# Three transformer layers on one core: loads moved between queues, a 16-row bias table, the ends of three mixers in another order, and no dummy products

## The reference

```python
def gmlp_mixer(x, ...):
    z = gelu(x @ w_in); u, v = split(z)
    v = layernorm(v, ln_g, ln_b)
    v = einsum('gpq,bnqgc->bnpgc', masked(w_s), v) + b_s
    return (u * v) @ w_out

def diff_attention(x, ...):
    s = q @ k.T * scale + rel_bias[t5_bucket(kpos - qpos)]   # two maps of each head
    attn = softmax(s0) - lam_full * softmax(s1)
    o = rmsnorm(attn @ v, sub_g) * (1 - lambda_init)
    return o @ w_out

def conv_ffn(x, ...):
    h = causal_dwconv(x @ w_up, conv_w, conv_b)
    return (gelu(h[..., :2816]) * h[..., 2816:]) @ w_down

for layer in (0, 1):
    h = h + rmsnorm(mixer(rmsnorm(h, g0)), g1)
    h = h + rmsnorm(conv_ffn(rmsnorm(h, g2)), g3)
x = h + 0.5 * swiglu(rms_norm(h))
x = x + concat(mla(...), moba(...)) @ w_out
x = x + 0.5 * swiglu(rms_norm(x))
return rms_norm(x)
```

## Time and profile before

| | before |
|---|---|
| median of 3 runs | 1166.54 us (1165.56 to 1166.56) |
| the profiled execution | 1168.31 us, its span 1166.1 us |
| mean granted clock of TensorE | 0.975 |
| PE, DVE, ACT, POOL busy | 94%, 63%, 52%, 3% of the span |
| read from DRAM | 195.35 MB, 170 GB/s over the span |

### The profile page before, as it was taken

The page is one execution under the profiler, slowest core; times in us unless marked ns, Lnnn a source line. Parts: engine busy times, 40 slices in busy tenths (PEclk is TensorE's granted clock), DMA queues, the critical chain, the costliest instruction groups (busy, mean ns, idle before and its releaser), DMA issues.

```text
span 1166.1 us, 18036 instructions
## 1 busy us (share of the span) xinstructions
PE 1096.7 (94%) x7308; PEld 1002.7 (86%) x7308; DVE 732.7 (63%) x1145; ACT 607.7 (52%) x1060; POOL 40.5 (3%) x47
## 2 busy tenths in 40 slices
PE   6989399999899898999999999999998989999997
PEld 4977399999789777999997999999897978999996
DVE  4865297767768875876767654555546845655453
ACT  6655166555756655655556543435453644543442
POOL 0720010000000000000000000000000000000000
PEclk9999699999999999999999999999998989999999
DMA  9742677565374234656554566565353422855540
GB/s 334 244 172 64 137 251 230 171 195 183 108 261 154 91 109 133 229 179 198 168 196 127 193 216 200 169 198 192 107 173 123 150 72 69 277 179 189 191 162 37
DMA packets 56081, 199.14 MB, mean 171 GB/s; under 512 B 6856, under 2 KB 7272, under 8 KB 56000
## 3 DMA queue, kind: packets, MB, share of 16 engines
q1 hardware_dynamic: 54000, 194.53, 50.2%
q0 software_dynamic: 1088, 2.63, 1.5%
q10 hardware_dynamic: 912, 0.84, 0.2%
HBM read 195.35 MB, written 2.62 MB: 170 GB/s over the span
## 4 chain that ended last, share of the span: by engine, by line
PE 85%; DVE 6%; ACT 4%; DMA 3%; issue 1%; ACTq 0%; DVEq 0%
PE Y L1242 26%; PE G L1207 15%; PE G L1209 15%; PE G L1208 15%; DMA raw<-in_panels 3%; DVE w_low L733 2%; PE G L1230 2%; PE G L1232 2%; PE G L1231 2%; ACT w_high L384 1%; PE G L1365 1%; PE Y L1254 1%; PE Y L1208 1%; PE Y L1207 1%; PE Y L1209 1%
## 5 line engine op out<-in xcount | busy, mean ns | idle before, releaser
L733 DVE TENSOR_TENSOR w_low<-raw,w_high 128x1024 fp32r<-128x1024 f32 x352 | 428.1, 1225 | 109.3 <-ACT w_high L384 108.0
L1207 PE MATMUL G<-x_parts,w_high 128*128 128x256 f32 x1504 | 429.7, 286 | 1.1 <-DVE w_low L733 1.1
L1208 PE MATMUL G<-x_parts,w_high 128*128 128x256 f32 x1504 | 427.9, 285 | 0.0
L1209 PE MATMUL G<-x_parts,w_low 128*128 128x256 f32 x1504 | 427.7, 284 | 0.0
L384 ACT CAST w_high<-raw 128x1024 fp32r<-128x1024 f32 x352 | 359.1, 1046 | 47.2 <-DMA raw<-in_panels 32.3
L1207 PEld LDWEIGHTS G<-x_parts,w_high 128*128 128x128 f32 x1504 | 290.6, 193 | 5.4 <-issue 2.1
L1208 PEld LDWEIGHTS G<-x_parts,w_high 128*128 128x128 f32 x1504 | 290.6, 193 | 2.9
L1209 PEld LDWEIGHTS G<-x_parts,w_low 128*128 128x128 f32 x1504 | 290.4, 193 | 0.0
L1242 PE MATMUL Y<-w_high,a_high 128*128 128x512 f32 x448 | 144.6, 405 | 25.4 <-DVE a_low L849 21.9
L1242 PE MATMUL Y<-w_high,a_low 128*128 128x512 f32 x448 | 142.2, 399 | 0.0
L1242 PE MATMUL Y<-w_low,a_high 128*128 128x512 f32 x448 | 141.6, 398 | 0.0
(11 more groups left out here) (211 smaller groups left out, 952.7 us busy)
## 6 DMA issues: line engine op xcount, KB each, us to landing
raw<-in_panels SPq DMA_DIRECT2D x352, 512.0 KB, 4.5
gain_pre<-in_gains SPq DMA_DIRECT2D x7, 512.0 KB, 5.6
gain_post<-in_gains SPq DMA_DIRECT2D x4, 512.0 KB, 6.8
rel_rows<-qk POOLq DMA_DIRECT2D x1, 1536.0 KB, 34.6
big<-in_xT SPq DMA_DIRECT2D x4, 256.0 KB, 9.0
h<-in_x SPq DMA_DIRECT2D x2, 512.0 KB, 13.8
big<-rel_rows POOLq DMA_DIRECT2D x8, 128.0 KB, 3.3
out_y<-w SPq DMA_DIRECT2D x4, 256.0 KB, 2.0
```

The source lines that it names most:

```text
L733: v.tensor_tensor(WL[:, n % RING, :], raw[:, n % RAWS, :], WH[:, n % RING, :].bitcast(F32), ALU.subtract).then_inc(lo, 1)
L1207: mm(out, WH[:, j, c:c + w], xh, start=first, stop=False, skip_group_check=skip)
L1208: mm(out, WH[:, j, c:c + w], xl, start=False, stop=False, skip_group_check=skip)
L1209: return mm(out, WL[:, j, c:c + w], xh, start=False, stop=last, skip_group_check=skip)
```

## The change

It does eight things. Loads: the six small loads move from ACT's queue to SP's, between the first panels; panel 5 comes ahead of `h`. Bias table: 16 rows a head, written by POOL as soon as `relt` is there and read back by SP in 8 pieces of 16 partitions, one behind every fourth panel of FFN0 from FFN0+6. FFN: the first `d` one pair of tiles later; conversions of panels +5 to +8 beside the `first2` copies; with the convolution a tile waits for `taps` and not for the product. Boundaries: panel +3 is converted within the boundary, except before FFN3, where it stays ahead. GMLP end: the mixing in two halves. DIFF end: norms of heads 0 to 3 ahead of `evac_qk(7)`, then those of 4 to 7 together; rows t=0 of heads 0 to 2 ahead of t=1. MIX: the evacuation and scores of pair 8 ahead of the rest, MoBA and MLA tiles one place later. No `warm`.

The parts stand in the order of the file: `_ffn_order`, SP, POOL, ACT (boundary, `first_two`, `ffn`, start, DIFF end), DVE (GMLP end, DIFF end, MIX), PE.

```diff
-        if 3 <= f < NF - 2:
-            seq.append(("d", f - 3))
+        if 4 <= f < NF - 1:
+            seq.append(("d", f - 4))
...
-        scratch = nc.dram_tensor("rel_rows", [HEADS, P * REL], F32)
+        scratch = nc.dram_tensor("rel_rows", [HEADS, 16 * REL], F32)
...
             load(4)
+            sp.dma_start(relw, io["rel"]).then_inc(rel_in, 16)
+            load(5)
             for t in range(TT):
                 sp.dma_start(h[:, t, :], io["x"][t]).then_inc(x_in[t], 16)
-            load(5), load(6)
+            load(6)
+            sp.dma_start(cst[:], io["consts"]).then_inc(cst_in, 16)
+            load(7)
             sp.dma_start(wsT, io["w_s"]).then_inc(ws_in, 16)
-            load(7)
+            sp.dma_start(par[:], io["params"]).then_inc(par_in, 16)
+            load(8)
             sp.dma_start(bsrow, io["b_s"].to_broadcast([P, D])).then_inc(ws_in, 16)
+            load(9)
+            sp.dma_start(posi[:, 0:T], io["pos_row"].to_broadcast([P, T])).then_inc(pos_in, 16)
+            sp.dma_start(posi[:, T:T + TT], io["pos_col"]).then_inc(pos_in, 16)
+            def table_rows(a):
+                src = bass.AP(scratch, P - 1 - 16 * a, [[REL - 1, 16], [16 * REL, HEADS], [1, T]])
+                sp.dma_start(bias[16 * a:16 * a + 16, :, P:SC], src).then_inc(rel_rd, 16)
...
+                if n == FFN0 + 2:
+                    sp.wait_ge(vp_r, 2)
+                    sp.wait_ge(rel_wr, 16)
+                    sp.dma_start(lamrow[:].rearrange("p a b -> p (a b)"),
+                                 io["lam"].to_broadcast([P, 4 * DIFF_D])).then_inc(lam_in, 16)
+                if n >= FFN0 + 6 and (n - FFN0 - 6) % 4 == 0 and n < FFN0 + 6 + 32:
+                    table_rows((n - FFN0 - 6) // 4)
                 load(n)
...
+            pool.wait_ge(relt_r, 1)
+            pool.dma_start(scratch_ap.rearrange("e (r c) -> e r c", c=REL),
+                           relt[:].unsqueeze(1).to_broadcast([HEADS, 16, REL])).then_inc(rel_wr, 16)
             pool.wait_ge(ws_in, 32)
...
-            pool.wait_ge(used, FFN0 + 4)
-            pool.dma_start(scratch_ap.rearrange("e (r c) -> e r c", c=REL),
-                           relt[:].unsqueeze(1).to_broadcast([HEADS, P, REL])).then_inc(rel_wr, 16)
-            pool.wait_ge(rel_wr, 16)
-            pool.wait_ge(vp_r, 1)
-            for e in range(HEADS):
-                src = bass.AP(scratch, e * P * REL + P - 1, [[REL - 1, P], [1, T]])
-                pool.dma_start(bias[:, e, P:SC], src).then_inc(rel_rd, 16)
-            pool.wait_ge(rel_rd, 16 * HEADS)
+            pool.wait_ge(rel_rd, 16 * 8)
...
+                upto(base + 3)
                 h_rms(b, 1)
...
                     s.copy(first2[:, t, :], G[:, t, :]).then_inc(fx_r, 1)
+                    upto(base + 7 + t)
...
-                upto(base + 5)
+                upto(base + 4)
-                upto(base + 3 * NF + 3)
+                upto(base + 3 * NF + 2)
...
-            upto(4)
+            upto(6)
             h_rms(0, 0)
-            upto(5)
             h_rms(0, 1)
             preload(ACT.Gelu_apprx_tanh)
             upto(9)
...
-                if k == HEADS - 1:
-                    rms_out(0, 5, 1)
-                    preload(ACT.Exp)
                 if k >= 1:
                     exps(k - 1)
                 if k >= 2:
                     last = squares_out(k - 2)
-                    if k == 6:
+                    if k == 5:
                         last.then_inc(ac, 1)
+                if k == 6:
+                    rms_out(0, 4, 1)
+                    preload(ACT.Exp)
             high_head(0), high_head(1)
+            turned_out(6, 0)
             exps(7)
-            turned_out(6, 0)
-            turned_out(7, 0)
+            high_head(2)
             squares_out(6)
             upto(DIFF + 31)
-            high_head(2)
+            turned_out(7, 0)
+            high_head(3)
             squares_out(7).then_inc(ac, 1)
-            rms_out(5, HEADS, 2)
+            rms_out(4, HEADS, 2)
...
+            mixed_in(0, 4)
             for k in range(4):
                 gate(k)
             for k in range(4):
                 a_low(k)
-            upto(21)
             scale_u(3)
+            mixed_in(4, KT)
             gate(4), gate(5)
+            upto(20)
             a_low(4), a_low(5)
             gate(6), gate(7)
+            upto(21)
             a_low(6), a_low(7)
...
+                if k == HEADS - 1:
+                    inverse_rms(0, 4, 1)
+                    for e in range(4):
+                        norm_head(e)
                 evac_qk(k, DIFF + 10 + 2 * k, DIFF_D ** -0.5)
-                upto(DIFF + 15 + 2 * k)
+                if k < HEADS - 1:
+                    upto(DIFF + 15 + 2 * k)
...
-                    inverse_rms(0, 5, 1)
-                    norm_head(0), norm_head(1)
                     head_values(5)
-                    combine(7)
...
+            combine(7)
             low_head(0), low_head(1)
+            head_values(6)
             weigh(7)
-            norm_head(2)
-            head_values(6)
+            low_head(2)
             upto(DIFF + 31)
             head_values(7)
-            norm_head(3), low_head(2), norm_head(4)
-            inverse_rms(5, HEADS, 2)
-            norm_head(5), norm_head(6), norm_head(7)
-            for e in range(3, HEADS):
+            low_head(3)
+            inverse_rms(4, HEADS, 2)
+            for e in range(4, HEADS):
+                norm_head(e)
+            for e in range(4, HEADS):
                 low_head(e)
                 upto(DIFF + min(29 + e, 34))
...
             upto(B + 14)
+            dve.wait_ge(dist_r, 1)
+            evac_qk(8, B + 12, DIFF_D ** -0.5)
             dve.wait_ge(cstd, 1)
...
-            upto(B + 15)
             dve.wait_ge(tab_r, 1)
             dve.wait_ge(kr_ps, 1)
...
+            combine(8)
+            upto(B + 16)
+            evac_qk(9, B + 14, DIFF_D ** -0.5)
             dve.wait_ge(cbc, 1)
             v.tensor_tensor(CR, facq[:], PB[:, 0:T], ALU.mult)
-            link(v.tensor_copy(rkv[0:64, :], PB[0:64, T:2 * T]))
+            v.tensor_copy(rkv[0:64, :], PB[0:64, T:2 * T]).then_inc(cb_r, 1)
+            dve.wait_ge(cb_r, 1)
+            weigh(8)
             upto(B + 17)
-            dve.wait_ge(dist_r, 1)
-            evac_qk(8, B + 12, DIFF_D ** -0.5)
-            upto(B + 19)
-            evac_qk(9, B + 14, DIFF_D ** -0.5)
-            combine(8)
...
-                warm(WARM)
...
-                            pe.wait_ge(pr, ph * NF + f - 3)
+                            pe.wait_ge(taps if ph < 2 else pr, ph * NF + f - 3)
...
-                if k == 0:
-                    pe.wait_ge(u_r, 4)
-                rows(GMLP + 16 + k, k, 1, k == 0, False)
+            pe.wait_ge(u_r, 4)
+            for k in range(3):
+                rows(GMLP + 16 + k, k, 1, k == 0, False)
...
             scores(7)
             head_out(0), head_out(1)
             turn(6, 0)
+            pe.wait_ge(nm_r, HEADS - 1)
+            head_rows(0, 0), weigh_values(6, 0), head_out(2), head_rows(1, 0), head_rows(2, 0)
+            turn(7, 0), head_out(3)
+            pe.wait_ge(nm_r, HEADS)
+            head_rows(0, 1), weigh_values(7, 0), head_rows(1, 1), head_rows(2, 1)
...
             moba_pair(0)
             column_sums()
+            scores(8)
             moba_pair(1)
             column_factors()
-            scores(8)
-            moba_pair(2)
+            pe.wait_ge(cb_r, 1)
-            turn(8, 0), scores(9), turn(8, 1), weigh_values(8, 0), moba_pair(3), weigh_values(8, 1)
+            turn(8, 0), scores(9), turn(8, 1), weigh_values(8, 0), moba_pair(2), weigh_values(8, 1)
```

More of the change, by code:

```diff
@@ L43 @@
 REL = 384
-WARM = 6
 GMLP = 0
@@ L579, in _ @@
             gate_u(3)
-            for k in range(4, KT):
-                high_s(k)
+            high_s(4), high_s(5)
+            upto(22)
+            high_s(6), high_s(7)
             upto(23)
@@ L586, in _ @@
             preload(ACT.Sqrt)
-            upto(FFN0 + 3)
+            upto(FFN0 + 2)
             boundary(1, ACT.Gelu_apprx_tanh)
@@ L689, in _ @@
             cast(8)
-            upto(B + 22)
+            upto(B + 21)
             exps(10)
@@ L983, in a_low, with mixed_in @@
                 v.tensor_tensor(AL[:, k, :], sg[:, k, :], AH[:, k, :].bitcast(F32), ALU.subtract).then_inc(al, 1)
-            dve.wait_ge(m_r, 4)
-            for k in range(KT):
-                last = v.scalar_tensor_tensor(
-                    out=sg[:, k, :].rearrange("p (n t) -> p n t", n=2),
-                    in0=mixed[:, k, :].rearrange("p (n t) -> p n t", n=2),
-                    scalar=par[:, C_LNG + k:C_LNG + k + 1], in1=spread(off[:, k, :], 2),
-                    op0=ALU.mult, op1=ALU.add)
-            last.then_inc(vp_r, 1)
-            dve.wait_ge(vp_r, 1)
+            def mixed_in(k0, k1):
+                for k in range(k0, k1):
+                    last = v.scalar_tensor_tensor(
```

(24 more changed lines are left out.)

98 lines of the change are left out of this document (43 added, 55 removed).

## The result

| | before | after |
|---|---|---|
| median | 1166.55 us (1165.56 to 1167.24, 4 runs) | 1126.46 us (1125.67 to 1128.47, 4 runs) |
| profiled execution, its span | 1168.31, 1166.1 us | 1125.67, 1123.9 us |
| mean granted clock | 0.975 | 0.990 |

The account below looks back on a forecast made before the run. TensorE, busy 94% of the span, was taken as the bound, so its waits and clock decide. Terms 27.4 + 4.4 + 5.8 - 3.0 + 5.5 - 1.2 = 38.9 us gave 1127.6 us, range 1115 to 1141.

Parts of the forecast that it names:

- The bias table: FFN0: the table write shrinks from 1536 to 192 KB, its 34.6 us become 4.3, ending the 17.9 us PE wait.
- rival (c): Table write does not shrink with its bytes or hits the start's loads; stall moves there, +20, 1147.6 us; chance 0.08.
- rival (d): FFN0: table pieces on SP's queue hold the panels back, 8 x 2.9 us, giving 1151 us; chance 0.05.
- The FFN starts: Four FFN blocks: all 21.9 us of `a_low` waits and the half clock behind two go, table included; 27.4 us gained.
- GMLP end and MIX: GMLP end: 2.86 us wait and half clock go, 4.4 us; MIX middle: 3.9 us wait and half clock go, 5.5 us.
- The boundaries: Six boundaries: dropping dummies and moving panel +3 gains 5.8 us: 2.6 at 5 and 6, 2.1 at 1, 3, 4, 1.1 at 2.
- one panel less ahead of them: Boundary 2: ACT's three table loads have one panel less in front, some 1.5 us, making 1.1 us gained.
- the longest thin stretch will be at boundary 2, the 3.7 us with 1.32 busy kept 1.00: Boundary 2: about 3.9 us with 0.9 busy; a similar earlier stretch kept full clock, so no clock loss was charged.
- rival (b): Boundaries: without dummies the clock falls, 1.5 to 3 us each, some 12 at six, giving 1139.6 us; chance 0.10.
- The DIFF end: End of DIFF: turn copy behind two table loads idles PE 3 us, tail waits grow; 3.0 us lost.
- Rival (a): End of DIFF loses its waits as the FFN starts do, 8 us faster, 1119.6 us; chance 0.15.
- The start: Kernel start: first product 0.9 us earlier, panel 7's 0.4 earlier, but half clock costs 1.6; net 1.2 us lost.

Follow-up runs that it names:

- kernel 1: Changed kernel with the bias table written in its old size (128 rows a head, 1536 KB) at the new early place: 1140.56 us, +14.1.
- kernel 2: Changed kernel with the small table written at the old time, after PE used FFN0's fourth panel, and read back from FFN0+18: 1126.16 us.
- kernel 3: Changed kernel with the old FFN order, conversion places and PE wait for the product; the small table stays: 1136.72 us, +10.3.
- kernel 5: Changed kernel with the middle of MIX in its old order (pair 8's evacuation and scores late): 1132.14 us, +5.7.
- kernel 8: Changed kernel with six dummy products back at each of the six boundaries: 1130.83 us, +4.4.
- kernel 7: Changed kernel with six dummy products back at boundary 2 alone: 1127.2 us, no difference.
- kernel 9: Changed kernel with ACT's exponential for lambda moved behind boundary 2, two table loads fewer ahead of it: 1124.39 us, 2.1 faster.
- kernel 11: Changed kernel with old DIFF end, table row's copy behind the first norm, and lambda's exponential behind boundary 2: 1117.69 us, 8.8 faster.
- kernel 6: Changed kernel with the end of DIFF in its old order: 1124.63 us, 1.8 faster.
- kernel 10: Changed kernel with DVE's copy of the table row moved from ahead of the first norm to behind it: 1123.18 us, 3.3 faster.
- kernel 12: Kernel 11 with lambda's exponential back in front of boundary 2; old DIFF end and moved table-row copy stay: 1120.53 us.
- kernel 4: Changed kernel with the end of GMLP in its old order (eight `mixed` steps first, `scale_u(3)` behind the panels): 1131.23 us, +4.8.

## Why the prediction was right, point by point

**The bias table: right, mechanism shown.** The size makes the stall (kernel 1), not the place (kernel 2), so rival (c), the stall moving to the start, would have come true had the bytes not shrunk, with 14.1 us for its 20. The page "DMA: Bandwidth & Descriptors" of the Trainium skill (section "Rules for kernel authors") gives such a transfer 8 of 16 engines at most; the trace of kernel 1 agrees, with 38.1% of 36 us for this queue, below half. My own check of it, 17.3 against 17.2 us, was luck. The 42.0% of the earlier trace rows hold the reading back of the table too, which the same queue did; the 34.9 us up to it show 41.2%, 14.4 us. The pieces on SP's queue, rival (d), cost nothing: no PE wait for a panel is left in FFN0, and they landed in 6.1 us at the median.

**The FFN starts: right, undersized.** 27.4 was the term; FFN0 to FFN3 gave 30.4 by the landmarks, taking 1.3 for boundary 5. Of this the order accounts for 11.2 (the FFNs of kernel 3's profile; 10.3 in its time, as it gives 0.9 back at boundary 2), which leaves some 19 for the table, a difference and not a run: the large table in FFN0 with the new order was not tried. Missing in my sum were the two waits of 0.5 for `w_low` ahead of the tiles.

**GMLP end and MIX: right in place, the sizes partly luck**: 4.8 for 4.4 and 5.7 for 5.5 by the medians. The waits are those of the forecast (2.86 and 3.90), and the new wait on `cb_r` took 0.8 us for 0.9. But the clock behind them was not: at the end of GMLP it differs by execution and the median hits the middle of two pairs, and in MIX it paid 1.7 for 2.5 in kernel 5's profile, with another 1.7 behind the column sums.

**The boundaries: right for five, wrong for one.** Dummies back at all six cost 4.4 us. At 1, 3 and 4 the chain came 0.7 earlier, as worked out, and the profile of kernel 8 loses just that with the dummies back; what moving panel +3 has in it is argued, as no kernel put the panel back. At 2 the term was 1.1 and the stretch gave 0.46, and then the clock fell. The step that failed is "one panel less ahead of them". The panel with its wait is gone, but the new FFN order, a part of the same change, puts another in its place: the stretch of kernel 3 is 0.91 shorter, which with 0.46 makes 1.4. My two sections were each worked out as if the other were not there. My step "the longest thin stretch will be at boundary 2, the 3.7 us with 1.32 busy kept 1.00" failed too: 4.7 us with 1.41 busy did not, as rival (b) has it, at one boundary of six. But this cost 0.5 us in the profile, not the 1.5 to 3 of rival (b). Dummies did not help (kernels 7 and 8, one profile each). What did was to make the wait shorter, by ACT's table loads for one exponential (kernels 9 and 11) or by one panel (kernel 3). I had named these loads and not seen that two of the three could go. The rule of the page "TensorE: Matmul & The Clock Gate" of the Trainium skill (Part 1, The HAM clock gate) that activity releases the throttle is neither borne out nor contradicted by kernel 7, where the clock fell behind six dummies and 1.12 and 0.83 us of idle time.

**The DIFF end: right sign, and about right in size.** Its loss was 3.0 by my schedule. Undoing it gave 1.8 in kernel 6 and 2.7 between kernels 10 and 12, and the profiles differ by 2.5 in the mean. The landmarks' 3.94 hold 0.5 of the clock behind boundary 2, and 3.5 of the end, where this pair of profiles has 3.4 us of half clock before and 6.8 after. The turn copy waited as foreseen (2.85 for 3). The waits in the tail were fewer than my schedule had (2.0 us for 3.5). Rival (a) is refuted.

**The start: a loss as forecast, but twice as large.** It cost 2.3 us for 1.2. The first product came 0.47 earlier, not 0.9 (8.92 for 9.39), and that of panel 7 0.6 later, not 0.4 earlier (30.16 for 29.52). The wait ahead of panel 7 was 3.18 for 2.9 and the half clock cost 1.6, as predicted. But I had put that wait down to two norms and a table load. 2.1 us of it was DVE's copy of the table row, queued ahead of the norm's first step; I had costed what ACT does there, and not what DVE waits for. Kernel 10 shows it.

**The sum.** The profiled execution fell by 42.6 for my 38.9, the median by 40.1. The profile of before was 1.8 above its median, and that of after 0.8 below its own, so some 2.6 of the difference is execution against execution. That the sum came within 1.2 us of the median is in part luck: the start lost 1.1 more than its term and boundary 2 gave 0.6 less, and FFN0 to FFN3 gave 3.0 more. And the bounds of my terms add up to 18 us above and 16 below the forecast, not 22 and 21.

## What to carry to other kernels

Before filling a gap with dummy products, ask what the gap waits for: here the dummies cost 4.4 us over six boundaries and did not hold the clock at the one where PE waited, while it stayed up once a two-number exponential, or one panel, was out of the way. Two parts of one change can meet at a wait: what moved on ACT for the FFN took back most of what was gained at the boundary behind it. And half clock costs only what the next wait does not take up, at boundary 2 0.5 us of 1.7. The large write cost its bytes at both places tried; make such a write smaller before looking for a better place. When a small copy is put early on an engine "because its data is there", look at what waits behind it: one copy of 0.55 us was worth 3.3 us.

## What the runs showed of the hardware

I had not expected how much the clock varies between executions at places where the code is the same. Twelve profiles hold the new middle of MIX, with 20 products of one column (2.29 us) in the same place. Behind it five show half clock for 3.4 to 6.8 us (kernels 3, 7, 9, 10 and 12) and seven none, with no PE wait of 0.1 us or more in that place in the changed kernel. Both profiles with the old middle (before, from 866.1, and kernel 5) have it there too. Behind the wait of 2.46 us at boundary 2 all eight profiles that hold it have half clock (the changed kernel and 1, 2, 4, 5, 6, 10 and 12), three for about 3.4 us and five for 6.8. Counted to the first scores of DIFF, the three lost 0.0 to 0.5 us and the five 1.1 to 1.3, as the wait of 0.9 us that follows took up the rest. Kernels 7 and 8, with dummies in that wait, have 3.4 us of half clock each; kernel 3 (1.56 us) and kernels 9 and 11 (0.43) have none. The kernel before has none either, with its dummies and then 1.58 us of wait, so the wait alone does not decide it. At the end of DIFF the new order has 6.8 us of half clock in two profiles and 10.2 in eight. So one such stretch comes or goes in a pair of profiles, and can pass for the gain or loss of an edit. MIX is such a case, with 7.6 us of landmarks (8.9 less boundary 6) for the 5.7 of kernel 5: before had half clock at 866 us and after did not, 1.7 us. What makes the difference at equal code I have not settled. The page "TensorE: Matmul & The Clock Gate" of the Trainium skill (Part 1, The HAM clock gate) says that the activity monitor runs free of the program, by which the same gap could be seen in one execution and missed in another; no run here tests that.
